# The preparation of a delta-rule recurrence in another order: exponentials first, block inverses begun from PSUM, half of the products inside the solver

## The reference, cut to what matters

```
w = -softplus(-(w0 + tanh(wd) @ w_decay_up)) - 0.5
a = sigmoid(a0 + ad @ a_up);  g = sigmoid(gd) @ g_up
kk = normalised(k * k_k);     k = k * (1 + (a - 1) * k_a)
def step(state, (r, d, k, v, kk, a)):          # 256 times
    sa = state @ -kk
    state = state * d + outer(sa, kk * a) + outer(v, k)
    y = state @ r
```

## Time and profile before

| | |
|---|---|
| median of 3 runs | 1549.05 us (1544.57 to 1550.05) |
| profiled execution, its own time | 1550.17 us |
| its span (first to last instruction) | 1548.2 us |
| mean granted TensorE clock | 0.984 |
| TensorE busy | 1484.2 us, 96% |
| VectorE, ScalarE, GpSimd busy | 989.2, 796.8, 125.0 us |

### The profile page before, as it was taken

How to read it: one execution, slowest core, us unless ns; L and a number is a source line. 1 busy time by engine, 2 the same in 40 slices (tenths; PEclk the granted TensorE clock), 3 DMA queues, 4 the chain that set the end, 5 groups by cost and what they waited for, 6 DMA issues and landing times.

```text
span 1548.2 us, 38369 instructions
## 1 busy us (share of the span) xinstructions
PE 1484.2 (96%) x15685; PEld 1214.6 (78%) x15685; DVE 989.2 (64%) x1375; ACT 796.8 (51%) x1015; POOL 125.0 (8%) x70
## 2 busy tenths in 40 slices
PE   7998899999999999999999999989999999999998
PEld 6996877899999989999999899966555555555554
DVE  4596425166665456765533654667887787888786
ACT  5446216344333358734232446465676666676764
POOL 1221400001333000000311000000000000000000
PEclk9999989999999999999999999999999999999999
DMA  9567346655555535553123335369999999999994
GB/s 310 176 187 228 102 141 196 240 164 164 189 176 179 192 109 164 166 161 110 57 65 100 110 117 169 131 277 364 414 404 365 400 395 406 415 416 374 417 415 195
DMA packets 178595, 362.26 MB, mean 234 GB/s; under 512 B 9229, under 2 KB 137722, under 8 KB 161658
## 3 DMA queue, kind: packets, MB, share of 16 engines
q1 hardware_dynamic: 178426, 359.90, 64.0%
HBM read 355.03 MB, written 1.05 MB: 230 GB/s over the span
## 4 chain that ended last, share of the span: by engine, by line
PE 73%; DVE 6%; DMA 4%; ACT 4%; issue 2%; DVEq 1%; ACTq 0%; SPq 0%; POOLq 0%
PE psum L3305 10%; PE psum L372 8%; PE psum L373 8%; PE psum L376 8%; PE psum L3321 5%; DMA proj<-in_w_exp_up 4%; PE psum L697 4%; PE psum L3276 3%; PE psum L3358 3%; PE psum L569 3%; PE psum L505 2%; PE psum L506 2%; PE psum L507 2%; PE psum L547 1%; DVE ring L2525 1%
## 5 line engine op out<-in xcount | busy, mean ns | idle before, releaser
L372 PE MATMUL psum<-proj_r 128*128 128x256 f32 x1392 | 341.6, 286 | 3.9 <-ACT proj_r L336 3.9
L373 PE MATMUL psum<-proj_r 128*128 128x256 f32 x1392 | 339.0, 284 | 0.0
L341 DVE TENSOR_TENSOR ring_r<-ring,proj_r 128x2048 fp32r<-128x2048 f32 x94 | 226.6, 2412 | 151.9 <-ACT proj_r L336 151.0
L2525 DVE COPY ring<-proj 128x1024 f32 x374 | 237.3, 688 | 90.9 <-PE psum L3305 62.2
L372 PEld LDWEIGHTS psum<-proj_r 128*128 128x128 f32 x1392 | 268.0, 193 | 8.0 <-issue 6.9
L373 PEld LDWEIGHTS psum<-proj_r 128*128 128x128 f32 x1392 | 268.1, 193 | 0.1
L336 ACT ACTIVATE proj_r<-ring 128x2048 fp32r<-128x2048 f32 x93 | 177.5, 1909 | 103.5 <-PE psum L376 93.0
L1888 ACT ACTIVATE ring<-proj 128x1024 f32 x186 | 189.1, 1051 | 6.9 <-issue 4.3
L376 PE MATMUL psum<-proj_r,ring_r 128*128 128x256 f32 x1392 | 182.7, 284 | 2.6 <-DVE ring_r L341 2.6
L376 PEld LDWEIGHTS psum<-proj_r,ring_r 128*128 128x128 f32 x1392 | 174.6, 193 | 3.0 <-DVE ring_r L341 2.8
L3305 PE MATMUL psum<-ring,u 128*32 128x256 f32 x1488 | 115.0, 385 | 3.6 <-DVE ring L2525 3.2
(11 more groups left out here) (574 smaller groups left out, 2700.4 us busy)
## 6 DMA issues: line engine op xcount, KB each, us to landing
ring<-in_w_in SPq DMA_DIRECT2D x65, 1024.0 KB, 5.2
proj<-in_w_exp_gate SPq DMA_DIRECT2D x64, 1024.0 KB, 9.2
proj<-in_w_exp_up SPq DMA_DIRECT2D x64, 1024.0 KB, 10.3
proj<-in_w_exp_down SPq DMA_DIRECT2D x64, 1024.0 KB, 8.2
ring<-in_w_ada SPq DMA_DIRECT2D x24, 1024.0 KB, 7.9
ring<-in_w_ffn_in SPq DMA_DIRECT2D x22, 1024.0 KB, 5.1
ring<-in_w_ffn_out SPq DMA_DIRECT2D x11, 1024.0 KB, 5.0
ring<-in_w_out SPq DMA_DIRECT2D x8, 1024.0 KB, 5.1
```

What stands on the lines that cost most here:

```text
L341: dve.tensor_tensor(ring_r[:, at.slot, :], ring[:, at.slot, :], self.heads[at.buffer].bitcast(F32), ALU.subtract) \
L372: pe.matmul(dst, w, xh, start=start, stop=False, skip_group_check=True)
L373: pe.matmul(dst, w, xl, start=False, stop=False, skip_group_check=True)
L2525: ins = dve.tensor_copy(into_copy[k_half][j][:, kind * D:(kind + 1) * D], pieces[:, bass.ds((piece + kind) & 7, 1), of_half].rearrange("p ...
```

## The change

Six edits, all in the order of things:

1. **ScalarE in the preparation.** The load of the exponential's table and `e2` come before the four `k2` activations; the copy of `g_gate` comes behind the exponentials. The copies of modulation groups 0 and 1, six tiny instructions, move from the preparation to behind the barrier.
2. **VectorE in the preparation.** `cum_prev` and `carry` come before `kk * a_gate`. The eight instructions that write `ar` become two of 1024 elements.
3. **Products.** The b products go to banks 2 to 5. Only the b products stand before the solver. The k products of half 0 follow the first turned half (`meanwhile(-1)`), those of half 1 stand in level 1.
4. **Inverses.** `begin` reads the b products in PSUM, before any masking. Level 0's `levels` are written by VectorE from PSUM (`first_level`) and no longer by GpSimd. The masks of `prods_b` and of `prods_k`, half 0, follow, those of half 1 at level 1.
5. **Filling.** `MODS_LEVELS` goes from (2, 2, 2, 2, 0) to (0, 0, 3, 5, 0), and x of chunk 0 moves from level 0 to level 2. GpSimd's carry masks move from level 0 to 2, its bonus product from 1 to 3.
6. **SyncE.** The load of modulation chunk 12 also waits for `block_upd_made` 10, the first product of level 4, both halves. All later loads queue behind it.

The core of the diff:

```diff
-        MODS_LEVELS = (2, 2, 2, 2, 0)
+        MODS_LEVELS = (0, 0, 3, 5, 0)
...
                     self.products(pe, bank[g], inv_t[:, g], eye).then_inc(sig("blocks_turned"), 1)
+                    if g == 0:
+                        meanwhile(-1)
...
+            def first_level(self, dve, g, m_t):
+
+                dve.tensor_tensor(self.levels[:, g], m_t, spread(const("half_level1"), HEADS), ALU.mult).then_inc(sig("block_first_masked"), 1)
...
+                if (kind, i) == ("mod", 12):
+                    sp.wait_ge(*rwkv_solver.at("block_upd_made", 10))
...
+            act.activation(small[:, 250:251], const("ones")[:, 0:1], ACT.Exp)
+            act.wait_ge(*reached("cum_ready", 1))
+            act.activation(e2, cum, ACT.Exp, scale=-LOG_DECAY).then_inc(sig("exps"), 1)
             act.wait_ge(*reached("a_gate_ready", 4))
...
-            for m in range(RT):
-                dve.tensor_tensor(ar[:, m, :, 0, :], tiles(kk)[:, m], tiles(e3)[:, m], ALU.mult)
-                ins = dve.tensor_tensor(ar[:, m, :, 1, :], proj[:, T_R + m, :].rearrange("p (c t) -> p c t", c=TB), tiles(e1)[:, m], ALU.mult)
-            ins.then_inc(sig("ar_ready"), 1)
+            dve.tensor_tensor(ar[:, :, :, 0, :], tiles(kk), tiles(e3), ALU.mult)
+            dve.tensor_tensor(ar[:, :, :, 1, :], tiles(proj[:, T_R:T_R + RT, :]), tiles(e1), ALU.mult).then_inc(sig("ar_ready"), 1)
...
+            b_made = lambda ch: psum[:, 2 + 2 * ch:4 + 2 * ch, :].rearrange("p b (h x t) -> p (b h) x t", x=2, t=HD)[:, :, 0, :]
             for ch in range(TB):
-                mask(prods_b, 2 * ch, 0, ch)
-                dve.wait_ge(*reached("prods_masked", 2 * ch + 2))
-                rwkv_solver.begin(dve, link, ch)
+                dve.wait_ge(*reached("prods_made", ch + 1))
+                rwkv_solver.begin(dve, link, ch, b_made(ch))
             for ch in range(TB):
-                mask(prods_k, 4 + 2 * ch, 1, ch)
-            rwkv_solver.dve(dve)
+                rwkv_solver.first_level(dve, ch, b_made(ch))
+            for ch in range(TB):
+                mask(prods_b, 2 + 2 * ch, 0, ch)
+            mask(prods_k, 6, 1, 0)
...
             def between_levels(lv):
+                if lv == -1:
+                    pe.wait_ge(*reached("mod_copied", MOD_GROUPS[2]))
+                    products(k_til, 6, 0)
+                    return
                 if lv == 0:
+                    pe.wait_ge(*reached("prods_masked", 4))
+                if lv == 1:
+                    pe.wait_ge(*reached("prods_masked", 6))
+                    products(k_til, 6, 1)
+                if lv == 2:
                     pe.wait_ge(*reached("prods_masked", 8))
                     of_values(bank[6], 0, 0, range(2), True).then_inc(sig("x_made"), 1)
                 aside.modulate(pe, MODS_LEVELS[lv])
```

More of the change, by code:

```diff
@@ L762, in pool @@
                 for lv in range(5):
-                    for g in range(TB):
+                    for g in range(TB) if lv else ():
                         n = TB * lv + g
-                        if lv:
-                            pool.wait_ge(*self.at("block_upd_made", n - TB + 1))
-                        else:
+                        pool.wait_ge(*self.at("block_upd_made", n - TB + 1))
+                        if lv == 1:
                             pool.wait_ge(*self.masked(g))
@@ L1509, in _ @@
                 act.activation(k2[:, m, :], a_gate[:, m, :], ACT.Identity, scale=v("k_a", m), bias=one_less_ka[:, m:m + 1]).then_inc(sig("k2_scaled"), 1)
[L1510 to L1514, removed]
             act.activation(e1, cum, ACT.Exp, scale=LOG_DECAY).then_inc(sig("exps"), 1)
@@ L1518, in _ @@
             act.activation(carry, carry, ACT.Exp, scale=LOG_DECAY).then_inc(sig("exps"), 1)
+            act.wait_ge(*reached("lora_out", 2))
+            act.activation(g_gate, psum[:, 4:6, :].rearrange("p b (m t) -> p (b m) t", t=S), ACT.Copy).then_inc(sig("g_copied"), 1)
             act.wait_ge(*reached("v_turned", 2))
             act.activation(v_tok, psum[:, 0:2, :], ACT.Copy)
-            aside.copy_modulation(act, 1)
             act.wait_ge(*reached("bk_turned", 2))
@@ L1525, in _ @@
             act.activation(bk_tok_1[0:HD], psum[0:HD, 4:6, :], ACT.Copy)
+            st.end()
             aside.copy_modulation(act, 2)
-            st.end()
             act.wait_ge(*reached("k2_ready", 1))
@@ L2050, in _ @@
                .then_inc(sig("cum_ready"), 1)
+            dve.wait_ge(*reached("cum_ready", 1))
+            dve.tensor_tensor(carry, mid[:, :, 0:CHUNKS - 1], mid[:, :, 1:CHUNKS], ALU.add)
+            dve.tensor_tensor(cum_prev, cum, decay_log, ALU.subtract).then_inc(sig("cum_ready"), 1)
             dve.wait_ge(*reached("a_gate_ready", 4))
@@ L2296, in _ @@
                 dve.wait_ge(*reached("g_prods_ready", ch + 1))
-                g_solver.begin(dve, link, ch)
+                g_solver.begin(dve, link, ch, g_prods[:, ch, :, 0, :])
+                g_solver.first_level(dve, ch, g_prods[:, ch, :, 0, :])
             dve.wait_ge(*reached("eg_ready", 1))
@@ L2747, in _ @@
             for ch in range(TB):
-                products(b_til, 2 * ch, ch)
-            pe.wait_ge(*reached("mod_copied", MOD_GROUPS[2]))
-            for ch in range(TB):
-                products(k_til, 4 + 2 * ch, ch)
+                products(b_til, 2 + 2 * ch, ch)
             def between_levels(lv):
+                if lv == -1:
+                    pe.wait_ge(*reached("mod_copied", MOD_GROUPS[2]))
+                    products(k_til, 6, 0)
+                    return
                 if lv == 0:
+                    pe.wait_ge(*reached("prods_masked", 4))
+                if lv == 1:
+                    pe.wait_ge(*reached("prods_masked", 6))
+                    products(k_til, 6, 1)
+                if lv == 2:
                     pe.wait_ge(*reached("prods_masked", 8))
```

30 lines of the change are left out of this document (17 added, 13 removed).

## The result

The changed kernel takes 1546.34 us (median of 20 runs, 1538.37 to 1550.41), the kernel before 1550.12 us (20 runs, 1544.57 to 1556.01). The ratio of the two sets of runs is 0.9969, with an interval from 0.9956 to 0.9982: a gain of 4.8 us, between 2.8 and 6.8. The medians themselves are only 3.8 us apart. The time lies inside the range that was given, but the forecast change was 8.8 us, so about half of it came: 55% by the ratio, 43% by the medians. The sign was right. The gain stays inside the 0.5% that the prediction called "no change", the case that had 0.41.

What follows compares the result with a forecast made beforehand. TensorE, busy 96% of the span, was taken as the bound, with idle or half-clock places to win. 9.35 - 3.0 + 6.0 + 0.2 - 2.2 - 1.6 = 8.8 us, giving 1540.3 us, range 1535 to 1547.

Steps and rivals of the forecast that it cites:

- no change: Whole kernel: time within 0.5%, 7.7 us, of the kernel before; chance 0.41.
- Step 6a: Solver's start: late instruction blocks stop TensorE in half 0's k products and level 0's step; 2.2 us lost, bounds 0 and 5.
- Step 4: T to the end of chunk 0's first filling: stop and half clock go, a 2.1 us wait for chunk 13 comes; 6.0 us gained.
- T: The end of level 4's first product, at 189.24 in the profile before.
- Step 1: Preparation: ScalarE's new order lets the products start earlier; 2.1 us gained, assuming no table reload.
- Step 2: Solver's start: less waiting for VectorE lets level 0's step begin at 154.0; 7.2 us more gained.
- step 3: Inside the levels: half 1's k products, x of chunk 0 and two modulation steps come back; -3.0 us.
- rival of the late blocks: Solver's start: late blocks move there, charges at upper bounds, 5 + 4; gain only 3.6 us, 1545.5; chance 0.16.
- Step 6b: After the stops at the solver's start and the wait for chunk 13: clock can fall; 1.6 us lost, bounds 0 and 5.
- Step 5: Second solver: no GpSimd level-0 mask and a shorter L740 let the halves turn earlier; 0.2 us gained.
- rival "stop and half clock behind T stay": Behind T: the stop is not the burst's, so holding loads buys nothing; gain 4.4 us, 1544.7; chance 0.17.
- slower rival: Levels 0 to 3: clock stays low in pure 64-wide products, some 14 us more, 1554; chance 0.06.

Runs made afterwards that it cites:

- paced: Changed kernel with loads 9 to 12 each held until the first product of another level (1 to 4), instead of one hold for the burst; ratio to kernel before 0.9929.
- prep_paced: Kernel before with edits 1 and 2, and loads 10 to 12 held for first products of levels 1, 3 and 4; ratio to kernel before 0.9950.
- before_look1: Kernel before, unchanged, profiled once more; no timed ratio, 11.4 us from T to the filling.
- after_again: Changed kernel, unchanged, profiled and timed a second time; ratio to kernel before 0.9967.
- after_look: Changed kernel, unchanged, a third profile; no timed ratio, 13.6 us from T to the filling.
- hold_only: Kernel before with edit 6 alone, the load of chunk 12 and those behind it held; ratio to kernel before 0.9995.
- no_hold: Changed kernel without edit 6, so chunk 12's load goes out when its slot is free; ratio to kernel before 0.9968.
- paced_fill: As paced, but chunk 0's first filling moved behind its second, in one piece of eight modulation steps; 1534.73 us, ratio to kernel before 0.9878.
- paced_early: As paced, but all eight modulation steps in level 2 and chunks 12 and 13 meant to load one at a time inside level 3; ratio to kernel before 0.9912.
- before_look2: Kernel before, unchanged, a third profile; no timed ratio, 17.1 us from T to the filling.
- null: Kernel before, unchanged, timed against itself and profiled; ratio 1.0007.
- prep_again: Kernel before with edits 1 and 2 alone, the preparation's order, timed a second time; ratio to kernel before 0.9968.

## Why the prediction was right in sign and too large

It gave 8.8 us, and 4.8 came. The steps that failed are 6a and 4: the stops at the solver's start were priced at 2.2 us and took 3.72, and the stretch from T to the filling was priced at 6.0 us and gave 3.2. The means of the profiles give 5.6 us in all: 2.7 up to T, 3.2 from T to the filling and -0.3 behind it (one of three profiles has a further microsecond at half clock).

- **Step 1, 2.1 us:** right. It measured 2.47, and no table was reloaded.
- **Step 2, 7.2 us, and step 3, -3.0 us:** right as a price of the order, 4.2 us together, and 3.8 to the fourth filling or 4.2 up to T where nothing stopped TensorE (paced against prep_paced). Steps 1 to 3 together were priced at 6.35 up to T, and paced brings 7.0 (59.4 - 52.4), or 6.6 from the 59.0 of the profile that the prediction read. L745 took the 0.69 us priced.
- **Step 6a, "I take 2.2, a little under the middle":** this is the first step that failed, as a size. The mechanism was right and so, within a few records, were both places, but the stops are 0.78 + 2.94 = 3.72 us. The bound had been worked out at 1.5 + 3.5 = 5, from the end of the burst and the landing of a block. Nothing spoke for less than that but the lack of a visible stop in before, where TensorE waits for VectorE at that moment (a block was 6.8 us behind the last there too). On this term the rival of the late blocks, with its full 5, lay nearly as far off on the other side.
- **Step 4, "6.0 us":** this is the second, and the larger error, 2.8 us with the clock of the filling. Its base was wrong: 17.0 us from T to the filling were read as what the kernel does, but the half clock behind the stop does not come in every execution (before_look1 has 11.4), and the mean is 15.6. And the landing was read a little too well: chunk 13 was waited for by 2.27, 2.35 and 3.06 us where 2.1 were priced, and the filling behind it took 3.22, 1.91 and 3.59 us where it was priced at 1.84. The end came at T + 12.4 instead of T + 11.05. So 1.4 us of the error are the base and 1.4 the end. The removal of the stop itself, 2.17 us, was right.
- **Step 6b, 1.6 us for the clock:** right in kind. The clock fell behind both idle pieces in two of the changed kernel's three profiles and behind neither in after_again. A fall before 163 costs 1.6 us (57.2 against 55.6 up to T), and one in the filling 1.3 to 1.7 (3.22 and 3.59 against 1.91) and in after_look a further microsecond behind it. Over the three profiles that is 2.4 us on average; the filling's part is in the T + 12.4 already. Why it falls in one execution and not in the next was not tried.
- **Step 5, 0.2 us:** can't be told. L745 takes 0.69 us there too, for L740's 1.67, but the time between the recurrence and the expert phase does not change by anything that stands out of the scatter.
- **The rival "stop and half clock behind T stay":** refuted by hold_only and no_hold. Its time of 1544.7 came close to the measured gain for another reason.
- **The slower rival:** no whole level ran at half clock in any profile.

The account, with 6b's 1.6 halved between its two places: forecast were 6.35 - 2.2 - 0.8 up to T, and 6.0 - 0.8 + 0.2 behind it, 8.75. Measured were 2.7 up to T, which is the 7.0 of paced less 3.4 of further stops and some 1.0 of half clock, and 3.2 - 0.3 = 2.9 behind it, 5.6. The 0.8 us from there to the timed 4.8 are within its interval.

**What stays open.** The preparation alone was timed at 7.9 and 5.0 us below before (0.9949, 0.9968; the intervals reach down to 4.7 and 2.3), though its stretch shows 2.8 us up to T, and 4.7 to the fourth filling, where the clock fell in one of its two profiles and in three of the four of before. paced_fill, too, gained more as timed, 18.9 us, than the 13.1 of its stretch. Its one profile shows where: its span is 19.0 us below the mean of before, of which 13.1 lie in the stretch, 1.3 between the fourth filling and the expert phase, and 4.3 in the last phase (510.7 against a mean of 515.1). The four kernels with paced loads have 510.7 to 512.9 us there, and the other twelve profiles 509.6 to 518.3, mean 514.6. Whether an earlier schedule shortens the last phase or these are lucky draws, 16 profiles don't settle. By the timed ratios alone it is not shown that edits 3 to 6 bring anything on top of edits 1 and 2 (0.9969 and 0.9967 against 0.9949 and 0.9968). That they do with paced loads is shown by the stretches of one profile each; the intervals of the two timed ratios still overlap.

## What to carry to other kernels

Before TensorE's short instructions are packed closer, look at what the DMA queues hold at that moment: instructions come by the same DMA engines, and a burst of megabyte loads made them late, so here the denser start gained nothing up to T until the burst was spread. A load that is held back to protect one place must still be in time for its first user; moving that user was worth more here than moving the load (4.0 us of the stretch in paced_fill, 1.0 in paced_early). And where a stretch's length hangs on a clock that falls in some executions and not in others, read the base from several profiles before a gain is taken from it.

## What the runs showed that had not been expected

- The stops are repeatable to 0.07 us (0.78, 0.78, 0.85, 0.78 and 2.94, 2.94, 2.94, 2.93 in four profiles of two kernels), while the granted clock behind them is not. In before, before_look2 and null it stayed at 0.50, which is 1.2 GHz, for 10 us and more with TensorE busy throughout; in before_look1, behind the same stop (1.71 us), it stayed at 1.00, and so it did in prep_again behind 1.62 us. The stops behind T were longer where the clock fell (2.17, 2.44, 2.28, 2.43, 2.29) than where it didn't (1.71, 1.62); which of the two causes the other, or neither, was not tried.
- Loads of 1 MB one at a time are enough for a late block: 1.11 and 1.44 us in paced_early.
- Holding the burst back turned 2.2 us of stop into 2.3 to 3.2 us of waiting for chunk 13, so that the time changed only by what the clock did around it.
